# The tile of 32 sample tokens in output projection and embedding gate: 1024 output columns as four groups of 256 into four groups of 32 PSUM partitions

## The reference, cut to what matters

```python
def rmsnorm(x, g):
    y = xf * lax.rsqrt(jnp.mean(xf * xf, axis=-1, keepdims=True) + RMS_EPS)
    return (y * g.astype(jnp.float32)).astype(x.dtype)

    merged = (sigmoid(gate_a) * (y_a @ lp['w_branch_a']) + sigmoid(gate_b) * (y_b @ lp['w_branch_b']))
    x = x + (merged.astype(dt) @ lp['w_out']).astype(dt)          # output projection, 1024 x 1024
    h = rmsnorm(x, lp['norm_ffn'])
    x = x + hier_moe(h, ...)                                      # top-1 group of 4, top-2 of its 8 experts
    h = rmsnorm(x, lp['norm_ple'])
    ple = sigmoid(h @ lp['w_ple_gate']) * (p @ lp['w_ple_proj'])  # embedding gate, 1024 x 1024
    x = x + ple
y = rmsnorm(x, norm_final)                                        # for prompt and sample tokens
```

## Time and profile before

| | us |
|---|---|
| median of 3 runs | 1208.96 (1208.92 to 1209.25) |
| span of the profiled execution, first to last instruction | 1206.1 |
| the runs' median over that span | 2.9 |
| TensorE busy, matmul records | 1056.6 (88%) |
| VectorE busy | 358.3 (30%) |
| ScalarE busy | 195.1 (16%) |

### The profile page before, as it was taken

One profiled execution on the slowest core, in us unless ns is written; L12 is line 12 of the kernel. 1 busy time (PEld: TensorE's weight loads), 2 busy tenths in 40 slices (PEclk: granted clock), 3 DMA queues, 4 the chain that ended last, 5 costly groups with the idle time before them and its releaser, 6 DMA issues. The chain is left out here.

```text
span 1206.1 us, 11503 instructions
## 1 busy us (share of the span) xinstructions
PE 1056.6 (88%) x4475; PEld 617.6 (51%) x4475; DVE 358.3 (30%) x637; ACT 195.1 (16%) x357; POOL 140.5 (12%) x221
## 2 busy tenths in 40 slices
PE   3999999599599799959997649999999999994897
PEld 3877887487588656737434213333333333331442
DVE  3113903769034422153113600101010111111643
ACT  2132003100122102200101201111111111111233
POOL 0000063220210330000000230101010101001100
PEclk9999999899599988979999869999999999997899
DMA  8112121031300202160105935988888898857101
GB/s 226 53 53 70 58 82 59 17 88 54 87 2 2 54 18 58 60 236 10 45 0 217 362 106 185 312 303 306 307 302 310 299 312 298 307 179 266 47 28 46
DMA packets 128135, 175.56 MB, mean 146 GB/s; under 512 B 7450, under 2 KB 113286, under 8 KB 123797
## 3 DMA queue, kind: packets, MB, share of 16 engines
q1 hardware_dynamic: 119901, 144.66, 35.7%
q0 software_dynamic: 5632, 21.92, 6.2%
q10 hardware_dynamic: 2560, 8.39, 1.9%
HBM read 159.44 MB, written 19.89 MB: 149 GB/s over the span
## 5 line engine op out<-in xcount | busy, mean ns | idle before, releaser
L914 PE MATMUL PB<-hT,ring 128*128 128x272 f32 x1088 | 258.1, 399 | 0.0
L914 PEld LDWEIGHTS PB<-hT,ring 128*128 128x128 f32 x1088 | 209.8, 194 | 45.4 <-issue 0.3
L1754 PE MATMUL PB<-wexp,BIG 128*64 128x512 f32 x512 | 229.7, 602 | 0.9 <-DVE BIG L1607 0.8
L1754 PEld LDWEIGHTS PB<-wexp,BIG 128*64 128x64 f32 x512 | 68.2, 138 | 136.5 <-issue 133.3
L1773 PE MATMUL PQ<-wexp,BIG 128*64 128x512 f32 x256 | 116.7, 598 | 1.0 <-ACT BIG L1433 1.0
L1611 DVE TENSOR_TENSOR BIG<-BIG,PB 64x256 f32<-64x256 f32 x32 | 13.2, 413 | 335.3 <-ACT BIG L1429 335.3
L914 PE MATMUL PB<-pooled,ring 128*128 128x272 f32 x256 | 62.6, 404 | 9.9 <-DVE pooled L823 9.5
L1815 PE MATMUL PQ<-wexp,mhT 128*128 128x512 f32 (+1 forms) x160 | 70.6, 601 | 0.0
L1146 PE MATMUL PQ<-ARBK,merged 128*128 128x512 f32 (+1 forms) x160 | 69.1, 593 | 1.6 <-DVE merged L830 1.6
L1773 PEld LDWEIGHTS PQ<-wexp,BIG 128*64 128x64 f32 x256 | 32.5, 136 | 59.9 <-issue 56.7
L914 PEld LDWEIGHTS PB<-pooled,ring 128*128 128x128 f32 x256 | 50.1, 197 | 21.6 <-DVE pooled L823 10.2
(11 more groups left out here) (361 smaller groups left out, 993.3 us busy)
## 6 DMA issues: line engine op xcount, KB each, us to landing
wexp<-in_expert_gate SPq DMA_DIRECT2D x32, 1024.0 KB, 5.9
wexp<-in_expert_up SPq DMA_DIRECT2D x32, 1024.0 KB, 8.8
wexp<-in_expert_down SPq DMA_DIRECT2D x32, 1024.0 KB, 10.8
ring<-in_w_in SPq DMA_DIRECT2D x34, 512.0 KB, 4.1
yd<-BIG ACTq DMA_DIRECT2D x32, 256.0 KB, 6.1
BIG<-in_x_prompt SPq DMA_DIRECT2D x8, 512.0 KB, 12.0
ARBK<-in_w_out SPq DMA_DIRECT2D x1, 4096.0 KB, 13.8
wexp<-in_w_ple_gate SPq DMA_DIRECT2D x1, 4096.0 KB, 12.9
```

Of the source, the lines that this page charges most:

```text
L914: last = pe.matmul(PB[n % 2][:, h, 0:HT], w, x[:, h * HT:(h + 1) * HT], start=(k == 0), stop=(k == len(ops) - 1))
L1754: last = pe.matmul(bank[2 + x][0:CAP, :], xgT[x][:, k, :], gu[:, k, :], start=(k == 0), stop=(k == KD - 1))
```

## The change

In both stages the tile of sample tokens leaves the loop of halves. Its 1024 output columns are cut into four groups of 256. Each group's product goes into the same bank 4 and the same 256 columns of it, but into another 32 partitions: group c into partitions 32c to 32c + 31. TensorE runs the four groups inside the loop over k, and signals once, behind the last.

In the output projection VectorE adds the four parts one after another, each from its 32 partitions of PSUM to partitions 0 to 31 of `x0`; `x1_ready` then counts nine. In the gate ScalarE takes four sigmoids into `sgw`, the two buffers `sgp` as one of 1024 columns, and for that waits until the eighth embedding is added; VectorE multiplies and adds all 1024 columns in one instruction each. `last_norm(2)` and the norms behind it keep their order.

```diff
@@ -606,7 +606,7 @@
         act.wait_ge(states_stored, 32)
         for n in range(NTILE):
             r = ROWS[n]
-            act.wait_ge(x1_ready, 2 * n + 2)
+            act.wait_ge(x1_ready, min(2 * n + 2, 9))
             nc.scalar.activation(HN[0:r, n, :], x0[0:r, n, :], ACT.Square, accum_out=ss[0:r, n:n + 1]).then_inc(x1_squares_summed, 1)
             act.wait_ge(x1_mean_square_ready, n + 1)
             nc.scalar.activation(ss[0:r, n:n + 1], ss[0:r, n:n + 1], ACT.Sqrt).then_inc(x1_root_ready, 1)
@@ -839,14 +839,20 @@
             v.tensor_scalar(HN[0:r, n, :], x0[0:r, n, :], ss[0:r, n:n + 1], None, ALU.mult)
 
         dve.wait_ge(residual_loaded, 16 * NTILE)
-        for g in range(2 * NTILE):
+        for g in range(8):
             n, q = g // 2, g % 2
             dve.wait_ge(w_out_product, g + 1)
-            x = x0[0:ROWS[n], n, 512 * q:512 * q + 512]
-            v.tensor_tensor(x, x, bank[4 + g % 4][0:ROWS[n], :], ALU.add).then_inc(x1_ready, 1)
+            x = x0[0:P, n, 512 * q:512 * q + 512]
+            v.tensor_tensor(x, x, bank[4 + g % 4], ALU.add).then_inc(x1_ready, 1)
             if q and n:
                 norm_tile(n - 1)
-        norm_tile(NTILE - 1)
+        dve.wait_ge(w_out_product, 9)
+        for c in range(4):
+            x = x0[0:NSM, 4, 256 * c:256 * c + 256]
+            last = v.tensor_tensor(x, x, bank[4][NSM * c:NSM * c + NSM, 0:256], ALU.add)
+        last.then_inc(x1_ready, 1)
+        norm_tile(3)
+        norm_tile(4)
 
     @block.tensor
     def _(pe):
@@ -1137,14 +1143,18 @@
         pe.wait_ge(merged_ready, KD)
         pe.wait_ge(w_out_loaded, 16)
         pe.wait_ge(states_turned_taken, WT_N)
-        for g in range(2 * NTILE):
+        for g in range(8):
             n, q = g // 2, g % 2
-            r = ROWS[n]
             if g >= 4:
                 pe.wait_ge(x1_ready, g - 3)
             for k in range(KD):
-                last = pe.matmul(bank[4 + g % 4][0:r, :], merged[:, k, n * P:n * P + r], WO[:, k, 512 * q:512 * q + 512], start=(k == 0), stop=(k == KD - 1))
+                last = pe.matmul(bank[4 + g % 4], merged[:, k, n * P:n * P + P], WO[:, k, 512 * q:512 * q + 512], start=(k == 0), stop=(k == KD - 1))
             last.then_inc(w_out_product, 1)
+        pe.wait_ge(x1_ready, 5)
+        for k in range(KD):
+            for c in range(4):
+                last = pe.matmul(bank[4][NSM * c:NSM * c + NSM, 0:256], merged[:, k, NPR:T], WO[:, k, 256 * c:256 * c + 256], start=(k == 0), stop=(k == KD - 1))
+        last.then_inc(w_out_product, 1)
 
 
 E_ALL, G_ALL, EPG = 32, 4, 8
@@ -1253,6 +1263,7 @@
     sq = wf[:, KD * D + 6144:KD * D + 6144 + NTILE * 1024].rearrange("p (n d) -> p n d", n=NTILE)
     gf = wf[:, KD * D + 11264:KD * D + 12288]
     sgp = [wf[:, KD * D + 12288 + 512 * k:KD * D + 12800 + 512 * k] for k in range(2)]
+    sgw = wf[:, KD * D + 12288:KD * D + 13312]
     cst, wr, gffn, gple, bias = kept
     c_ = lambda name: cst[:, CONST2[name][0]:CONST2[name][0] + CONST2[name][1]]
     ident = c_("ident")
@@ -1483,17 +1494,23 @@
 
         def last_norm(n):
             r = ROWS[n]
-            act.wait_ge(S["emb_added"], 2 * n + 2)
+            act.wait_ge(S["emb_added"], min(2 * n + 2, 9))
             A_(sq[0:r, n, :], X1[0:r, n, :], ACT.Square, accum_out=ssq[0:r, n:n + 1]).then_inc(S["last_squares_summed"], 1)
             act.wait_ge(S["last_mean_square"], n + 1)
             A_(ssq[0:r, n:n + 1], ssq[0:r, n:n + 1], ACT.Sqrt).then_inc(S["last_root"], 1)
 
-        for n in range(NTILE):
+        for n in range(4):
             gate_sigmoid(2 * n)
             gate_sigmoid(2 * n + 1)
             if n:
                 last_norm(n - 1)
-        last_norm(NTILE - 1)
+        act.wait_ge(S["gate_ready"], 9)
+        act.wait_ge(S["emb_added"], 8)
+        for c in range(4):
+            last = A_(sgw[0:NSM, 256 * c:256 * c + 256], bank[4][NSM * c:NSM * c + NSM, 0:256], ACT.Sigmoid)
+        last.then_inc(S["gate_sigmoid_ready"], 1)
+        last_norm(3)
+        last_norm(4)
 
     @block.vector
     def _(dve):
@@ -1667,12 +1684,16 @@
             link(v.reciprocal(ssq[0:r, n:n + 1], ssq[0:r, n:n + 1]))
             v.scalar_tensor_tensor(X1[0:r, n, :], X1[0:r, n, :], ssq[0:r, n:n + 1], gf[0:r], ALU.mult, ALU.mult).then_inc(S["y_ready"], 1)
 
-        for n in range(NTILE):
+        for n in range(4):
             add_embedding(2 * n)
             add_embedding(2 * n + 1)
             if n:
                 last_norm(n - 1)
-        last_norm(NTILE - 1)
+        dve.wait_ge(S["gate_sigmoid_ready"], 9)
+        link(v.tensor_tensor(sgw[0:NSM], sgw[0:NSM], PP[0:NSM, 4, :], ALU.mult))
+        v.tensor_tensor(X1[0:NSM, 4, :], X1[0:NSM, 4, :], sgw[0:NSM], ALU.add).then_inc(S["emb_added"], 1)
+        last_norm(3)
+        last_norm(4)
 
     @block.tensor
     def _(pe):
@@ -1806,14 +1827,21 @@
                 last.then_inc(S["normed_turned"], 1)
 
         def gate(n):
-            r = ROWS[n]
             pe.wait_ge(S["normed_taken"], 2 * n + 2)
             for g in (2 * n, 2 * n + 1):
                 if g >= 4:
                     pe.wait_ge(S["gate_sigmoid_ready"], g - 3)
                 for k in range(KD):
-                    last = pe.matmul(bank[4 + g % 4][0:r, :], hT[:, k, n * P:n * P + r], WG[:, k, 512 * (g % 2):512 * (g % 2) + 512], start=(k == 0), stop=(k == KD - 1))
+                    last = pe.matmul(bank[4 + g % 4], hT[:, k, n * P:n * P + P], WG[:, k, 512 * (g % 2):512 * (g % 2) + 512], start=(k == 0), stop=(k == KD - 1))
                 last.then_inc(S["gate_ready"], 1)
+
+        def gate_samples():
+            pe.wait_ge(S["normed_taken"], 2 * NTILE)
+            pe.wait_ge(S["gate_sigmoid_ready"], 5)
+            for k in range(KD):
+                for c in range(4):
+                    last = pe.matmul(bank[4][NSM * c:NSM * c + NSM, 0:256], hT[:, k, NPR:T], WG[:, k, 256 * c:256 * c + 256], start=(k == 0), stop=(k == KD - 1))
+            last.then_inc(S["gate_ready"], 1)
 
         turn_normed(0)
         turn_normed(1)
@@ -1826,7 +1854,7 @@
         turn_normed(4)
         gate(2)
         gate(3)
-        gate(4)
+        gate_samples()
 
 
 def program(nc, a, o):
```

## The result

The changed kernel takes 1190.66 us, the median of 4 runs (1187.61 to 1193.29), where the kernel before took 1208.94: a ratio of 0.9855, 95% interval 0.9834 to 0.9876. The forecast was 1191.3. The profiled execution has a span of 1189.6 us (before: 1206.1).

A forecast was written before the change was run, and what follows sets the result against it. TensorE was taken to bound the gate's stage until the sample tile's last product. Stages of -9.2 and -8.5 gave -17.7 us, span 1206.1 to 1188.4; with 2.9 from span to median, 1191.3 us, range 1189 to 1197.5.

The forecast's parts named there:

- Four partition groups run as two do: Sample tile on TensorE, both stages: four groups side by side, 3.65 us a stage instead of 13.9; chance 0.76.
- Weight loads cost nothing: TensorE, sample tile: 64 loads of 0.11 us a stage cost nothing; rival, loads between matmuls, 1194.0 us, chance 0.05.
- Tail of the projection: Output projection's end on VectorE: four adds of 32x256, 1.69 us instead of 0.61, so 1.08 more.
- Start of the gate's tail, 0.9 late behind the table load: Gate's end: TensorE done at 1186.95, sigmoids start at 1187.87 after their table load, 9.39 us earlier than before.
- Tail of the gate from the first sigmoid: Gate's end: four sigmoids 0.28 apart, multiply and add of 1.22 us each; +0.89 us, sigmoids' upper end +0.4 more.
- Stage sums: Output projection -9.2 us (-9.5 to -9.0), embedding gate -8.5 us (-8.7 to -8.1).
- The clock, no difference taken: Half-clock stretches behind 644 may fall differently on TensorE's moved work: no difference taken, 1.5 us to either side.
- Order of issue: Sample tile on TensorE: four matmuls for each k, overlap resting on partition groups; no term for issue order.

The follow-up runs named there:

- order_by_group: Changed kernel with the loops exchanged, groups outside and k inside, still four partition groups: 1205.73 us, ratio 0.9977 to the kernel before.
- order_by_two_k: Changed kernel issuing two matmuls (four records) of one group, then two of the next, and so on: 1191.25 us, one run.
- one_partition_group: Changed kernel with all four products in partitions 0 to 31 of banks 4 and 5, groups outside and k inside: 1209.54 us, ratio 1.0013 to before.

## Why the prediction was right, point by point

- *Four partition groups run as two do.* Right, and shown to be the cause: one group 14.0 us, two 7.06, four 3.66. With the groups' order of issue as in the first of these, four take 11.5, so the order is part of the cause (last point).
- *Weight loads cost nothing.* Right: 64 of them in 2.0 us of busy time beside the matmuls. The rule of the Trainium skill ("TensorE: Matmul & The Clock Gate", Part 3, The mechanism) that loads overlap matmuls in flight only when the row group differs does not hold in these traces. It did not before the change either, with one partition group: there a load starts at 626.349 beside the record that runs from 626.348 to 626.940.
- *Tail of the projection*, forecast +1.08: measured +1.04 from TensorE's end to the end of the last scaling (3.43 before, 4.47 after). The adds were 0.42 apart, not 0.45.
- *Start of the gate's tail, 0.9 late behind the table load.* Right, and shown by moving the load.
- *Tail of the gate from the first sigmoid*, forecast +0.89 with +1.29 as the upper end: measured 7.63 against 6.43, +1.20. The term that was too small is the sigmoids: 0.39 apart and not 0.28. I took the spacing from two copies that read the same partitions; with a change of partitions it did not come out (0.39, and 0.26 to 0.28 without one).
- *Stage sums* -9.2 and -8.5: measured -9.2 and -8.2 in the profiled executions, and the same in the changed kernel's three other traces (9.78 and 14.59 to 14.60 us).
- *The clock, no difference taken.* Between the stages the profiled execution lost nothing by it, -0.35; the changed kernel's three other traces have -0.37, +1.43 and -0.38. But I allowed 1.5 us to either side, after three runs of before that lay 0.3 us apart; single runs lie 10 us apart over 38, most of it with the clock, so that a median of four can be off by a microsecond or two. So it is partly luck that the result lies within 0.7 us of the forecast. The better test is over all runs: 1191.1 (19) against 1209.1 (38), -18.0 where -17.7 was forecast.
- *Order of issue.* I took the groups' overlap as a property of the groups alone. It also needs an order in which the groups come in turn, as in the change with the loop over groups inside that over k; with the loops exchanged most of the gain is lost, 11.5 us in a stage and 1205.73 in all. The change had the right order, but the prediction gave no reason for it.

## What to carry to other kernels

A tile of 32 tokens stands in the profile as 128*32 where one of 128 tokens is 128*128, and in one partition group its matmuls take as long (593 ns a record for both): cut its output columns into four and send each part to its own 32 PSUM partitions, with the parts issued in turn, so that no more than three records of one part wait. (This case shows it for f32, where a matmul is two records.) The four parts then come out of PSUM in four small instructions, here each starting only when the one before was done; count them, and look for what ScalarE does at that moment, since a table load that was hidden can be the next wait. Judge changes of a few us by stage lengths in the trace where the clock moves the whole time by 10 us.

## What was not expected of the hardware

- TensorE took up records of another partition group past waiting ones, with up to three waiting for each group (order_by_group: the next group's first record starts with the 13th of 16; order_by_two_k: four groups with three waiting each, 3.73 us).
- ScalarE, like VectorE, started an instruction before the one ahead had ended where both read the same group of partitions, and not where they read different ones: the sigmoids 0.26 to 0.28 us apart (one_partition_group) against 0.39 (after).
- The same kernel on one core took from 1204.1 to 1214.3 us over 38 runs on two chips (about 9 us on each), at about 1 us for 0.001 of mean granted clock.
